# Building the expert gate matrices with accumulating indirect DMAs instead of one-hot matrix products

## What is computed

```
q = (xb @ w_query).reshape(PEER_BLOCK, PEER_HEADS, 2, PEER_HALF)
s = jnp.einsum("thpd,hpkd->thpk", q, sub_keys)
s1, i1 = lax.top_k(s[:, :, 0], PEER_TOPK)
s2, i2 = lax.top_k(s[:, :, 1], PEER_TOPK)
cand = (s1[..., :, None] + s2[..., None, :]).reshape(PEER_BLOCK, PEER_HEADS, PEER_TOPK * PEER_TOPK)
sc, flat = lax.top_k(cand, PEER_TOPK)
e = i1[flat // PEER_TOPK] * N_KEYS + i2[flat % PEER_TOPK]        # per token and head
g = jax.nn.softmax(sc, axis=-1)
a = jax.nn.gelu(jnp.einsum("thkd,td->thk", u_emb[e], xb))
return jnp.einsum("thk,thkd->td", g * a, v_emb[e])
```

## Time and profile before

| | us |
|---|---|
| median of three runs | 3485.08 |
| span of the profiled execution (first to last instruction) | 3486.2 |
| TensorE busy | 3400.2 (98%) |
| TensorE weight load busy | 2951.7 |
| VectorE busy | 2360.2 |
| ScalarE busy | 1221.5 |
| GpSimd busy | 1194.6 |

### The profile page before, as it was taken

How to read it: one execution, slowest core, us unless ns; L and a number is a source line. 1 busy time by engine, 2 the same in 40 slices (tenths; PEclk the granted TensorE clock), 3 DMA queues, 4 the chain that set the end, 5 groups by cost and what they waited for, 6 DMA issues and landing times.

```text
span 3486.2 us, 47324 instructions
## 1 busy us (share of the span) xinstructions
PE 3400.2 (98%) x18196; PEld 2951.7 (85%) x18196; DVE 2360.2 (68%) x4309; ACT 1221.5 (35%) x1635; POOL 1194.6 (34%) x746
## 2 busy tenths in 40 slices
PE   7999889999999999999999989999999999999998
PEld 3886578888888889999999768888888888999998
DVE  6777720994487724998997330895477723999997
ACT  3216633333455532222223333333355532222222
POOL 0000033454100002776772453454200002877761
PEclk9999989999999999999999999999999999999999
DMA  7771030344455556999995230344455555999995
GB/s 284 260 252 49 25 145 1 127 145 145 160 191 222 198 180 219 365 359 366 384 376 210 73 122 12 110 146 145 159 206 186 222 183 202 357 370 361 359 361 198
DMA packets 286132, 735.16 MB, mean 211 GB/s; under 512 B 33362, under 2 KB 116947, under 8 KB 266196
## 3 DMA queue, kind: packets, MB, share of 16 engines
q1 hardware_dynamic: 203988, 530.63, 43.1%
q0 software_dynamic: 45056, 134.38, 10.3%
q10 hardware_dynamic: 36864, 67.13, 5.0%
HBM read 612.48 MB, written 119.54 MB: 210 GB/s over the span
## 4 chain that ended last, share of the span: by engine, by line
PE 93%; POOL 2%; DVE 2%; DMA 1%; ACT 1%; issue 1%; SPq 0%; DVEq 0%; POOLq 0%; ACTq 0%
PE ps L1373 40%; PE ps L1411 28%; PE ps L1175 5%; PE ps L1326 5%; PE ps L1277 5%; PE ps L1386 3%; PE ps L1203 2%; PE ps L1235 1%; POOL picked L1496 1%; PE ps L1215 1%; PE ps L1318 1%; PE ps L1129 1%; PE ps L1089 0%; POOL ring_lo L1484 0%; DMA modall<-in_w_mod 0%
## 5 line engine op out<-in xcount | busy, mean ns | idle before, releaser
L1373 PE MATMUL ps<-xhi,Uhi 128*128 128x512 f32 x2048 | 807.5, 394 | 0.0
L1373 PE MATMUL ps<-xhi,Ulo 128*128 128x512 f32 x2048 | 798.4, 390 | 0.0
L1373 PE MATMUL ps<-xlo,Uhi 128*128 128x512 f32 x2048 | 796.6, 389 | 0.0
L1496 POOL DMA_INDIRECT picked<-act_scratch,aidx x256 | 381.9, 1492 | 985.0 <-DMA act_scratch<-act_st 907.6
L1411 PE MATMUL ps<-Hhi,Vhi 128*128 128x384 f32 x2048 | 687.3, 336 | 6.7 <-DVE Hlo L2003 6.7
L1411 PE MATMUL ps<-Hlo,Vhi 128*128 128x384 f32 x2048 | 685.9, 335 | 0.0
L1411 PE MATMUL ps<-Hhi,Vlo 128*128 128x384 f32 x2048 | 685.8, 335 | 0.0
L1027 ACT CAST Vhi<-Vraw 128x1024 fp32r<-128x1024 f32 x256 | 269.8, 1054 | 787.0 <-PE ps L1411 766.4
L986 ACT ACTIVATE act_st<-ps 128x512 f32<-128x512 f32 x256 | 153.1, 598 | 869.6 <-PE ps L1373 535.1
L1373 PEld LDWEIGHTS ps<-xhi,Ulo 128*128 128x128 f32 x2048 | 384.3, 188 | 82.2
L1373 PEld LDWEIGHTS ps<-xlo,Uhi 128*128 128x128 f32 x2048 | 384.9, 188 | 77.6
(11 more groups left out here) (283 smaller groups left out, 4547.1 us busy)
## 6 DMA issues: line engine op xcount, KB each, us to landing
Uraw<-in_UT SPq DMA_DIRECT2D x128, 1024.0 KB, 5.7
Vraw<-in_V SPq DMA_DIRECT2D x256, 512.0 KB, 5.7
act_scratch<-act_st ACTq DMA_DIRECT2D x256, 256.0 KB, 5.5
G_scratch<-G_st SPq DMA_DIRECT2D x24, 2048.0 KB, 8.2
act<-act_scratch SPq DMA_DIRECT2D x256, 192.0 KB, 6.0
Gin<-G_scratch SPq DMA_DIRECT2D x192, 256.0 KB
modw<-in_w_mod SPq DMA_DIRECT2D x80, 512.0 KB, 4.8
ring<-in_query SPq DMA_DIRECT2D x8, 2048.0 KB, 8.0
```

What stands on the lines that cost most here:

```text
L1373: mm = nc.tensor.matmul(up_bank(m), w, x[:, k, :], start=(k == 0 and j == 0), stop=(k == KT - 1 and j == 2))
L1496: nc.gpsimd.indirect_dma_start(picked[:, :, :].rearrange("p h k -> p (h k)")[:, p:p + 1], None, act_dram[layer].rearrange("m p (t o) -> (m ...
```

## The change

- The one-hot matrices, their products, the transposes of the picks and ScalarE's copies are gone, with the stores of G_st.
- G is now a DRAM tensor for each layer, indexed by expert and token (column count 384). It is set to zero by 16 DMAs of 1.5 MB a layer from a small zero tile. For layer 0 they stand in SyncE's queue during the attention, behind the second load of the attention's bias table. For layer 1 they stand in the up stage of layer 0, one behind each of the U loads at m = 41, 43 to 71.
- `put_gates` on GpSimd then issues 3 x 128 = 384 indirect DMAs a layer. Each adds, for one pair number and one tile, 128 weights (one for each token) to 128 places of 4 bytes in G. An added wait makes each group of 16 (one head of one tile) wait until the earlier groups of its tile have landed, since two heads of a token can choose the same expert. `PUTS` interleaves the tiles.
- Tiles are routed in the order 1, 2, 3, 0. VectorE takes the remainders of U from m = 13 on, one at each of 14 points inside `picks` of the second to fourth tile.
- The loads of G wait for all puts. They are 192 KB each, one a step, four steps ahead.

```diff
-TOK = 8
-HOTS_AT = 56
-REST_AT = HOTS_AT + 1
-EXP_AT = {13: 0, 25: 1, 37: 2, 49: 3}
-TURN_AT = {40: 1, 51: 2, 53: 3}
+ROUTE = (1, 2, 3, 0)
+REST_AT = 13
+POINTS = 14
+EXP_AT = {11: 0, 26: 1, 40: 2, 54: 3}
+WEIGHTS_AT = 56
+PUTS = ((0, 0), (0, 1), (0, 2), (1, 0), (0, 3), (1, 1), (0, 4), (2, 0), (1, 2), (0, 5), (2, 1), (1, 3),
+        (0, 6), (2, 2), (1, 4), (0, 7), (2, 3), (1, 5), (2, 4), (1, 6), (2, 5), (1, 7), (2, 6), (2, 7))
+NZ = 3 * P // 2
+ZROWS = 16
+ZERO_AT = 40
...
+            def zero_gates(layer, n):
+                flat = G_dram[layer].rearrange("m p t -> (m p t)").rearrange("(p n z) -> p n z", p=P, z=NZ)
+                sp.dma_start(flat[:, n * ZROWS:(n + 1) * ZROWS, :],
+                             zeros[:, :].unsqueeze(1).to_broadcast([P, ZROWS, NZ])).then_inc(G_zeroed, 16)
...
+                if h == 1:
+                    sp.wait_ge(zeros_ready, 1)
+                    for n in range(NZERO):
+                        zero_gates(0, n)
...
+                    if layer == 0 and ZERO_AT <= m < ZERO_AT + 2 * NZERO and m % 2 == 1:
+                        zero_gates(1, (m - ZERO_AT) // 2)
...
-                for n in range(2):
-                    sp.wait_ge(G_stored[n], 16 * (layer + 1) * NCHT // 2)
-                for c in range(0, NCHT, GPIECE):
-                    load_gates(layer, 0, c, c + GPIECE)
+                for r in range(1, TT):
+                    sp.wait_ge(G_put[r], 16 * NPK * (layer + 1))
+                load_gates(layer, 0)
+                load_gates(layer, 1)
...
-                    for b in batches_after(m):
-                        gates_out(b)
...
-                    if m in TURN_AT:
-                        turn_picks(TURN_AT[m])
-                    for b in batches_after(m):
-                        gate_weights(b)
...
+            def put_gates(layer):
+                pool.wait_ge(G_zeroed, 16 * NZERO * (layer + 1))
+                for order, h in PUTS:
+                    r = ROUTE[order]
+                    if h == 0:
+                        pool.wait_ge(pick_ready, layer * TT + order + 1)
+                    at_least(pool, G_put[r], 16 * (layer * NPK + h * TOPK))
+                    for k in range(TOPK):
+                        nc.gpsimd.indirect_dma_start(
+                            G_dram[layer].rearrange("m p (t o) -> (m p t) o", o=1),
+                            bass.IndirectOffsetOnAxis(ap=gidx[r][:, h * TOPK + k:h * TOPK + k + 1], axis=0),
+                            pick[r][:, 3, h, k:k + 1], None, compute_op=ALU.add).then_inc(G_put[r], 16)
...
             peer_rests(0)
+            put_gates(0)
             peer_rows(0)
```

More of the change, by code:

```diff
@@ L198, in backbone @@
         picked = sb("picked", 188.5, [P, PH, TOPK])
-        row_no = sb("row_no", 22.625, [P, 1])
+        row_no = sb("row_no", 22.625, [P, TT])
+        gidx = [sb(f"gidx{r}", 187.5 + 2 * r, [P, NPK], U32) for r in range(TT)]
+        zeros = sb("zeros", 206, [P, NZ])
         act_st = [sb("act_st0", 196, [P, T]), sb("act_st1", 20, [P, T])]
@@ L426, in backbone @@
         H_step = sem("H_step")
[L427 to L431, removed]
+        zeros_ready = sem("zeros_ready")
+        G_zeroed = sem("G_zeroed")
+        G_put = [sem(f"G_put{r}") for r in range(TT)]
         act_done = sem("act_done")
@@ L453, in backbone @@
         V_in = [sem(f"V_in{n}") for n in range(NVRAW)]
-        G_in = [sem(f"G_in{n}") for n in range(2)]
+        G_in = [sem(f"G_in{n}") for n in range(4)]
         U_hi = sem("U_hi")
@@ L1531, in _ @@
             peer_rests(1)
+            put_gates(1)
             peer_rows(1)
@@ L1803, in peer_route, with rest_of_U, picks, between @@
             def peer_route(layer):
-                def picks(r):
+                def rest_of_U(m):
+                    slot, cols = pair_of(m)
+                    dve.wait_ge(U_hi, layer * NW + HP + m + 1)
+                    nc.vector.tensor_tensor(Ulo[slot][:, :, cols], Uraw[slot][:, :, cols],
+                                            Uhi[(HP + m) % 3][:, :, :].bitcast(F32), ALU.subtract).then_inc(U_rest, 1)
+                def picks(order):
+                    r = ROUTE[order]
                     chosen = pick[r]
+                    def between(point):
+                        if order >= 1 and point is not None:
+                            rest_of_U(REST_AT + (order - 1) * POINTS + point)
                     carry_wait()
-                    def top16(rows, vals, ids, src):
+                    def top16(rows, vals, ids, src, points):
                         for i in rows:
@@ L1813, in top16 @@
                         step(last)
+                        between(points[0])
                         carry_wait()
@@ L1817, in top16 @@
                         step(last)
+                        between(points[1])
                         carry_wait()
@@ L1881, in picks @@
[L1881 to L1889 removed]
+                    step(nc.vector.scalar_tensor_tensor(out=key1[:, :, :], in0=key1[:, :, :], scalar=float(NKEY),
+                                                        in1=chosen[:, 2, :, :], op0=ALU.mult, op1=ALU.add))
@@ L1890, in weights @@
+                def weights(order):
+                    chosen = pick[ROUTE[order]]
+                    dve.wait_ge(gate_exp, layer * TT + order + 1)
                     step(nc.vector.tensor_reduce(zsum[:, 0, :], chosen[:, 3, :, :], AX, ALU.add))
```

225 lines of the change are left out of this document (47 added, 178 removed).

## The result

The changed kernel takes 3706.55 us (median of four runs, 3703.76 to 3710.07), the kernel before beside it 3485.27 us: a ratio of 1.0638, 95% interval 1.0623 to 1.0653. It is 221.3 us slower, where 89 us faster was forecast. The profiled execution has a span of 3708.3 us.

What follows compares the result with a forecast made beforehand. TensorE, 93% of the chain, was taken to bound the kernel. 3485.1 - 98.5 (products) + 2 (zeros before the bias) + 8 (activation stores) = 3396.6 us, called 3396; whole range 3382 to 3560 us.

Steps and rivals of the forecast that it cites:

- The price of a put: Up stage, GpSimd: each put was taken to cost 1.40 us, range 1.24 to 2.13 us, judged from gathers of 128 values.
- break-even of 1.635 us: Up stage: price a put at which late puts on GpSimd use up the layer's gain of 49 us.
- Rival 1: Puts on GpSimd end after the up stage and delay the dense stage, 3535 to 3865 us; chance 0.22.
- its two cases: Puts at 1.70 us, ending 771 us after up starts: 3535 us; at 2.13 us, ending at 936 us: 3865 us.
- The products: Up stages, TensorE: dropping one-hot products and transposes leaves bare steps of 5.44 us, gaining 98.5 us in all.
- rival 4: Up stages: the one-hot products were free, something else paces steps at 6.45 us, time stays 3485 us; chance 0.03.
- The scale by VectorE's busy share: Up stage: a put's price on GpSimd was set by how busy VectorE is, 1.24 us lowest, 2.13 us where packed.
- The other page's rule: Puts in the up stage: an add needs two source reads and two read descriptors a piece; spoke for slower puts.
- Zeros before the bias: Layer 0's attention: zeros in SyncE's queue end at 347 us, ahead of the third bias load; 2 us for queueing.
- Stores of activations: Layer 0's up stage: layer 1's zeros crowd SyncE's queue and delay these stores' landings; 8 us taken, ends 0 and 82.
- Remainders on VectorE: Up stage: 44 remainders a layer moved to VectorE fit beside the picks, the tightest 4.8 us early; cost nothing.
- a margin of 17%: Up stage: distance from the 1.40 us taken for a put on GpSimd to the 1.635 us where the gain is gone.

## Why the prediction was wrong

- **The price of a put: the step that failed.** The prediction took 1.40 us from gathers and argued that "GpSimd's price is that of naming 128 places". The addition costs GpSimd itself about 0.6 us more: 1548 against 958 ns at the median, put against plain put, and 0.57 us a put in the time of the kernel in which 96 puts lose it (55 / 96). With 0.30 us between puts the floor is 1.85 us, above the break-even of 1.635 us. That decided the sign. But at the price it took the forecast wouldn't have held either: plain puts, every 1.26 us, brought the crawl and 4140 us, which neither its sum nor its rivals had. Puts get longer while the other engines work: 1.55 us of GpSimd's time each where they stand still, 1.68 us (169.44 / 101) in the up stage; which operations do it is told under VectorE's busy share. These are two stretches of the changed kernel:

```profile
900.00:1100.00 200.00, 196.33 (x857) 161.53 (x856) 46.13 (x44) 58.22 (x75) 169.44 (x101) 0.99 0.86 219
...
1310.00:1460.00 150.00, 4.63 (x21) 3.51 (x19) 0.00 (x0) 1.36 (x2) 123.92 (x81) 0.52 0.25 6
```

  Rival 1 happened, in size between its two cases: at 1.97 us its own sum is 86 + 384 x 1.97 + 18 + 14 = 874 us, 128 us late in each layer, 3741 us. It was 3706.55 us, 34 us less. The waits for landings were 7.7 us a layer instead of 18, and the start of the dense stage took 8.6 us after the last put instead of 14: 2 x 15.7 = 31 us of that.
- **How much lies in the gaps.** Without puts the change gives -93.6 us. TensorE's wait for H is 312.3 us longer with them (320.2 against 7.9). 3485.3 - 93.6 + 312.3 = 3704.0 us; 2.6 us are left. While TensorE stands in the gap the granted clock is at 0.52, its level of 1.2 GHz, and the first products of the dense stage still run at it:

```profile
1470.00:1480.00 10.00, 9.69 (x46) 9.72 (x47) 7.93 (x14) 2.11 (x2) 7.87 (x8) 0.79 1.01 386
1480.00:1500.00 20.00, 20.00 (x117) 20.00 (x116) 12.32 (x20) 5.27 (x5) 13.94 (x13) 1.00 0.96 350
```

  The 45 products in the chain take 9.82 us, where at the pace of the second stretch they would take 7.7: some 2 us in this layer, so the clock is enough for what is left.
- **The products: right.** 96.9 us of 98.5 were seen in the stages of the kernel without puts, none was free (rival 4).
- **The scale by VectorE's busy share: the wrong measure of a real effect.** From 760 to 900 us VectorE is busy for 111.06 of 140 us and a put takes 115.65 / 68 = 1.70 us; from 900 to 1100 us, with VectorE at 46.13 of 200 us, 1.68 us. Put by put the trace shows what lengthens them. GpSimd's and VectorE's timelines:

```profile
1008.45 1.55 POOL L1433 DMA_INDIRECT G_scratch<-pick,gidx  x1 [0.30 <-issue]
1010.30 2.52 POOL L1433 DMA_INDIRECT G_scratch<-pick,gidx  x1 [0.30 <-issue]
1013.12 2.55 POOL L1433 DMA_INDIRECT G_scratch<-pick,gidx  x1 [0.30 <-issue]
```

```profile
1010.17 1.23 DVE L1754 TENSOR_TENSOR Ulo<-Uraw,Uhi 128x1024 fp32r<-128x1024 f32 x1 [5.30 <-ACT Uhi L940]
1013.02 1.23 DVE L1754 TENSOR_TENSOR Ulo<-Uraw,Uhi 128x1024 fp32r<-128x1024 f32 x1 [1.62 <-ACT Uhi L940]
```

  The put of 1010.30 us starts 1.10 us before the remainder ends and takes 0.97 us more than its floor. Of the 201 puts that start from 900 to 1300 us, 44 are longer than 1.60 us. All 44 start while a remainder runs, and each is longer by the rest of that remainder less 0.13 us; only 3 short ones start with over 0.2 us of a remainder left. These 44 make up the whole distance from 1.55 us to the mean. During `picks` the two operations on eq do the same, while puts that start beside FIND_INDEX8, MATCH_REPLACE8 or TENSOR_REDUCE stay at 1.55 us. So what counts is how often a put starts beside a TENSOR_TENSOR, not how busy VectorE is. The rule weighed from the Trainium skill, "SBUF — State Buffer", "Who interferes with whom", counted copy, cast and tensor_scalar alone, and by it a put had the lowest price from m = 55 on. The trace doesn't agree: the operations beside which puts got longer there are remainders.
- **The other page's rule pointed the right way.** That an add needs two source reads and two read descriptors ("Collectives: The Full Stack" of the Trainium skill, "The bandwidth ceiling: the fold count and why AG ≠ RS ≠ AR") stood beside rival 1. The trace has it as packets of GpSimd's DMA queue. Over the whole run it has 45,056 in the kernel without puts, 69,632 with plain puts, 106,496 with additions on 64 partitions and 155,648 with additions on 128. Divided by 768 puts that is 32 packets for a plain put, 80 for an addition of 64 values and 144 for one of 128: one for each value and 16 more. So the trace agrees that an addition needs more, and here it is 4.5 times as much. In 1310 to 1460 us the packets of 81 puts are:

```profile
q0 software_dynamic: 11520, 0.05, 23.6%
```

  They take 23.6% of 16 x 150 us, 7.0 us of one engine a put; 0.3 us was foreseen. The rival was given 0.22. Whether GpSimd's 0.6 us more is the writing of these packets isn't shown: 64 fewer take off 0.15 us, and at that rate the 112 more than a plain put has would be 0.26 us.
- **Zeros before the bias: nothing.** The third bias table is loaded at 350.08 us and used at 355.04 us, against 349.22 and 354.10, both 0.9 us later. The zeros' last DMA is issued at 338 us; the DMA engines are full to 345 us (the view counts a share of 1.07) and at 0.08 from 345 to 350 us. So the prediction's 347 us was near, and the zeros were out of the way just before the load. In the changed kernel, SyncE's queue and VectorE's timeline:

```profile
265.99 72.25 SPq L643 DMA_DIRECT2D G_scratch<-zeros  x16
350.08 0.37 SPq L651 DMA_DIRECT2D btab<-in_btab  x1
```

```profile
355.04 0.69 DVE L1637 SCALAR_TENSOR_TENSOR btab<-btab,mask 128x512 f32<-128x512 f32 x1
```

- **Stores of activations: the right mechanism, smaller.** 8 us were taken. Layer 0's stage without puts is 699.0 - 696.4 = 2.6 us longer than layer 1's, which has no zeros beside it, and its chain runs over these stores. The change without puts lacks 98.5 - 93.6 = 4.9 us in all.
- **Remainders on VectorE: nearly right.** Cost nothing was forecast. TensorE waits for Ulo once, 2.4 us in the kernel without puts and 3.3 us in the changed one.

## What to carry to other kernels

An operation that the trace doesn't show has a price of its own even if a relative of it stands there a hundred times; where the price times the count decides the sign, as 384 puts with a margin of 17% did here, the price of its nearest relation is no centre for the forecast: here the bound from above, 2.13 us, was nearer to the measured 1.97 us than the 1.40 us taken. A stage hides a queue of work only up to a price that can be worked out from the trace before anything is built (1.53 us a put; near it the runs met it within 2 us a layer; further out it gave up to some 20 us too much, partly since the waits for landings were shorter than it took). Then move just as much as fits, here two tiles of three, and keep the old way for the rest.

## What the runs showed that was not expected

- An indirect DMA of 128 single values costs GpSimd 0.96 us as a store, 0.94 us as a gather and 1.55 us with an addition; 64 values with the addition cost 1.40 us. Another 0.30 us go by before the next.
- Long runs of plain indirect DMAs, one every 1.26 us with nothing of GpSimd's own between, bring all other engines to a crawl: TensorE made 124 products in 330 us, with no wait that the profile names. A memset of 0.12 us before each and a wait for it ended that, 4140 us against 3398 us. The additions, at 1.85 us or more, never showed it, and it began only after some ten plain ones in a row at their floor. What the engines share there stays open.
- A put is at its floor or, with few exceptions, starts beside a two-input VectorE operation and waits for its end: with 128x8 memsets the median is 963 ns and the mean 1134 ns. All 62 long puts of that kernel from 900 to 1290 us start beside a remainder.
- An addition makes one packet for each value and 16 more in GpSimd's DMA queue (144 for 128 values), where a store or a gather of 128 values makes 32.
